# A hybrid attention, gMLP and mixture-of-experts step on one core: expert matrices laid row beside row on a partition

## What is computed

```python
def _hier_moe(h, router_group, router_expert, w_gate, w_up, w_down):
    t = h.reshape(B * L, D)                       # 640 tokens in all
    g_top, g_idx = lax.top_k(softmax(t @ router_group), 1)
    e_top, e_idx = lax.top_k(<expert logits of that group>, 2)
    weights = softmax(e_top) * g_top
    gates = <weights at the two chosen experts, 0 elsewhere>     # (640, 32)
    # w_gate, w_up: (32, 1024, 256)   w_down: (32, 256, 1024)
    hid = silu(einsum('td,edf->tef', t, w_gate)) * einsum('td,edf->tef', t, w_up)
    y = einsum('tef,efd->td', hid * gates[:, :, None], w_down)
```

## Time and profile before

| | |
|---|---|
| median of 3 runs | 660.07 us (659.71 to 664.84) |
| the profiled execution, its own time | 659.92 us |
| its span, first to last instruction | 658.1 us |
| TensorE matmul busy | 544.3 us (83%) |
| VectorE, ScalarE, POOL busy | 188.8, 151.6, 175.6 us |
| DMA | 173.15 MB in 53935 packets, mean 263 GB/s |
| mean granted TensorE clock | 0.957 of full speed |

### The profile page before, as it was taken

How to read it: one execution, slowest core, us unless ns; L and a number is a source line. 1 busy time by engine, 2 the same in 40 slices (tenths; PEclk the granted TensorE clock), 3 DMA queues, 4 the chain that set the end, 5 groups by cost and what they waited for, 6 DMA issues and landing times.

```text
span 658.1 us, 9133 instructions
## 1 busy us (share of the span) xinstructions
PE 544.3 (83%) x3051; PEld 297.7 (45%) x3051; DVE 188.8 (29%) x571; ACT 151.6 (23%) x374; POOL 175.6 (27%) x242
## 2 busy tenths in 40 slices
PE   0479999999988788999997889899998778897700
PEld 0235654444445455455553446465654334454400
DVE  1150222001176765144447411111111111111027
ACT  1630102001106655122223011111111111111133
POOL 1000000002422433033334533343343222221204
PEclk9999999999997999999999899999999898899965
DMA  7999207136099500442146799999999999999368
GB/s 238 405 403 397 107 1 271 49 122 262 1 264 410 223 2 1 168 165 82 65 169 246 262 346 394 409 407 412 403 397 404 389 393 397 400 413 411 142 276 218
DMA packets 53935, 173.15 MB, mean 263 GB/s; under 512 B 7740, under 2 KB 8420, under 8 KB 52976
## 3 DMA queue, kind: packets, MB, share of 16 engines
q1 hardware_dynamic: 45680, 153.88, 60.9%
q0 software_dynamic: 7184, 15.70, 7.3%
q10 hardware_dynamic: 1008, 2.75, 1.0%
HBM read 163.75 MB, written 16.68 MB: 274 GB/s over the span
## 4 chain that ended last, share of the span: by engine, by line
PE 46%; DMA 36%; DVE 7%; SPq 3%; ACT 3%; issue 3%; POOL 1%; POOLq 0%; DVEq 0%; ACTq 0%
DMA ring<-in_w_down_dram 17%; PE ps L714 11%; PE ps L611 10%; PE ps L592 5%; PE ps L513 5%; DMA w<-in_w_down_dram 5%; DMA w_6d<-in_w_down_dram 4%; PE ps L531 3%; PE ps L593 3%; DMA w_7d<-in_w_down_dram 2%; PE ps L861 2%; DMA ring<-in_w_mod_dram 2%; PE ps L691 2%; DMA ring<-in_w_up_dram 2%; SPq L424 2%
## 5 line engine op out<-in xcount | busy, mean ns | idle before, releaser
L861 PE MATMUL ps<-ring,xt 128*64 128x256 f32 x704 | 84.1, 393 | 14.6 <-DMA ring<-in_w_up_dram 9.5
L861 PEld LDWEIGHTS ps<-ring,xt 128*64 128x64 f32 x704 | 55.7, 141 | 49.2 <-DMA ring<-in_w_up_dram 15.7
L611 PE MATMUL ps<-ring,h_t 128*128 128x512 f32 x160 | 69.5, 593 | 0.0
L1354 DVE TENSOR_TENSOR hid<-act_g,ps 128x128 f32<-128x128 f32 x32 | 9.2, 288 | 196.6 <-ACT act_g L1572 196.6
L861 PE MATMUL ps<-w,xt 128*64 128x256 f32 x416 | 51.5, 401 | 10.5 <-DMA w<-in_w_up_dram 7.5
L714 PE MATMUL ps<-ring,mix_t 128*128 128x512 f32 x120 | 53.6, 596 | 0.0
L1698 POOL DMA_INDIRECT expert_results<-y_sb,idx_out x32 | 32.8, 1024 | 59.0 <-ACT y_sb L1586 49.8
L861 PEld LDWEIGHTS ps<-w,xt 128*64 128x64 f32 x416 | 33.6, 144 | 32.7 <-DMA w<-in_w_up_dram 12.2
L611 PEld LDWEIGHTS ps<-ring,h_t 128*128 128x128 f32 x160 | 30.1, 190 | 37.6 <-issue 37.6
L592 PE MATMUL ps<-ring,h_t 128*128 128x512 f32 x80 | 42.0, 607 | 2.7 <-DVE h_t L1013 2.7
L1629 POOL TENSOR_TENSOR gm_stats<-gm_stats,half_pow 128x8 f32<-128x8 f32 x5 | 9.7, 1941 | 129.4 <-DVE gm_stats L1079 129.4
(11 more groups left out here) (239 smaller groups left out, 723.9 us busy)
## 6 DMA issues: line engine op xcount, KB each, us to landing
ring<-in_w_mod_dram SPq DMA_DIRECT2D x8, 3072.0 KB, 19.6
ring<-in_w_gate_dram SPq DMA_DIRECT2D x20, 1024.0 KB
ring<-in_w_up_dram SPq DMA_DIRECT2D x20, 1024.0 KB
ring<-in_w_down_dram SPq DMA_DIRECT2D x20, 1024.0 KB
w<-in_w_gate_dram SPq DMA_DIRECT2D x12, 1024.0 KB
w<-in_w_up_dram SPq DMA_DIRECT2D x12, 1024.0 KB
y_back<-expert_results SPq DMA_DIRECT2D x5, 1024.0 KB, 8.7
ring<-in_w_in_dram SPq DMA_DIRECT2D x2, 2048.0 KB, 17.7
```

The costliest lines, as they stand in the source:

```text
L611: last = pe.matmul(ps[:, 4 + u % 4, :], h_t[:, k, i * P:(i + 1) * P], w[:, k, :], start=(k == 0), stop=(k == KC - 1))
L861: last = pe.matmul(bank[fh * SLOT:(fh + 1) * SLOT, 0:FE].rearrange("p (a f) -> p a f", a=2), x_t[:, k % 4, (k // 4) * SLOT:(k // 4 + 1) * ...
```

## The change

All three matrices of an expert are loaded as `(p k)`: partition p gets eight neighbouring rows of gate and of up (8p to 8p+7), and two neighbouring rows of down (2p and 2p+1), each in one run of 8 KB. Since partition p of chunk c of w_down is now row 2p+c, the hidden units are split into even and odd instead of first and second half: gate_up reads every second column. Chunk k of the model dimension is now every eighth, so `turn_x` takes every eighth column of a whole row. Tokens are gathered as whole rows: 64 indices, 4 KB each, on partitions 0 to 63 or 64 to 127 (four buffers in one tile of two rows; the fourth is that of the extra tiles). `turn_x` has eight transposes of 64 partitions x 128 columns. The buffers of the expert results change their places.

```diff
-        xg = sb("xg", [P, XS, 512], F32, a0)
-        xt = sb("xt", [P, 2, 4, P], F32, a0 + 6 * KB)
+        xg = sb("xg", [P, 2, D], F32, a0)
+        xt = sb("xt", [P, 2, KC, SLOT], F32, a0 + 8 * KB)
...
-        y_sb = sb("y_sb", [P, 2, 512], F32, a0 + 13 * KB)
+        y_sb = sb("y_sb", [P, 512], F32, a0 + 15 * KB)
...
-        xg_x = sb("xg_x", [P, 512], F32, b0 + 40 * KB)
-        y_sb2 = sb("y_sb2", [P, 512], F32, b0 + 42 * KB)
+        y_sb2 = sb("y_sb2", [P, 2, 512], F32, b0 + 40 * KB)
...
+        def x_rows(j):
+            return slice(SLOT * (j % 2), SLOT * (j % 2 + 1))
+        def x_buf(j):
+            return xg[x_rows(j), j // 2, :]
...
             def load_half(e, a):
-                sp.dma_start(weights(e)[0][:, a].rearrange("p (h k) f -> p h (k f)", h=2),
-                             (w_gate, w_up)[a][0, e].rearrange("(h p k) f -> p h (k f)", h=2, p=P)
+                sp.dma_start(weights(e)[0][:, a].rearrange("p k f -> p (k f)"),
+                             (w_gate, w_up)[a][0, e].rearrange("(p k) f -> p (k f)", p=P)
                              ).then_inc(wgu_in[e % LS], 16)
             def load_down(e):
-                sp.dma_start(weights(e)[1], w_down[0, e].rearrange("(k p) f -> p k f", p=P)).then_inc(wd_in[e % LS], 16)
+                sp.dma_start(weights(e)[1].rearrange("p k f -> p (k f)"), w_down[0, e].rearrange("(p k) f -> p (k f)", p=P)).then_inc(wd_in[e % LS], 16)
...
-            def turn_x(src, bank, done):
-                columns = src.rearrange("p (q k) -> p k q", k=4)
-                for cc in range(4):
-                    last = transpose(bank[:, cc * P:(cc + 1) * P], columns[:, cc])
+            def turn_x(j, bank, done):
+                columns = x_buf(j).rearrange("p (q k) -> p k q", k=KC)
+                for k in range(KC):
+                    last = pe.matmul(bank[:, k * SLOT:(k + 1) * SLOT], columns[:, k], ident[x_rows(j), x_rows(j)],
+                                     is_transpose=True, start=True, stop=True)
...
             def gate_up(x_t, w, bank, done):
                 for k in range(KC):
                     for fh in range(2):
                         last = pe.matmul(bank[fh * SLOT:(fh + 1) * SLOT, 0:FE].rearrange("p (a f) -> p a f", a=2),
-                                         x_t[:, k % 4, (k // 4) * SLOT:(k // 4 + 1) * SLOT],
-                                         w[:, :, k, fh * P:(fh + 1) * P], start=(k == 0), stop=(k == KC - 1))
+                                         x_t[:, k], w.rearrange("p a k (f c) -> p a k f c", c=2)[:, :, k, :, fh], start=(k == 0), stop=(k == KC - 1))
...
+            def token_index(dst, src):
+                return dve.tensor_scalar(dst, src, 1.0, float(NO_CODE), ALU.mult, ALU.add)
             dve.wait_ge(r_idx, 1)
-            row_index(idx_in[:, :, 0], ps[:, 6, 0:XS]).then_inc(rows_made, 1)
+            token_index(idx_in[:, :, 0], ps[:, 6, 0:XS]).then_inc(rows_made, 1)
...
             def gather(e):
                 j = e % XS
                 if e >= XS:
-                    pool.tensor_copy(idx_in[:, j, 0:1], src_row[:, e:e + 1]).then_inc(idx_cp, 1)
+                    pool.tensor_copy(idx_in[0:SLOT, j, 0:1], src_row[0:SLOT, e:e + 1]).then_inc(idx_cp, 1)
                     pool.wait_ge(idx_cp, e + 1 - XS)
-                pool.indirect_dma_start(xg[:, j, :], None, h2_halves,
-                                        bass.IndirectOffsetOnAxis(ap=idx_in[:, j, 0:1], axis=0),
-                                        bounds_check=2 * TILES * P - 1, oob_is_err=False).then_inc(xg_in[j], 16)
+                pool.indirect_dma_start(x_buf(j), None, h2_dram,
+                                        bass.IndirectOffsetOnAxis(ap=idx_in[0:SLOT, j, 0:1], axis=0),
+                                        bounds_check=TILES * P - 1, oob_is_err=False).then_inc(xg_in[j], 16)
...
-            pool.memset(xg_x[:], 0.0).then_inc(xg_zero, 1)
+            pool.memset(x_buf(XS), 0.0).then_inc(xg_zero, 1)
```

More of the change, by code:

```diff
@@ L169, in hybrid_dit_step @@
         mix_t = sb("mix_t", [P, KC, TILES * P], F32, a0)
-        xg = sb("xg", [P, XS, 512], F32, a0)
-        xt = sb("xt", [P, 2, 4, P], F32, a0 + 6 * KB)
-        act_g = sb("act_g", [P, 2, P], F32, a0 + 10 * KB)
-        hid = sb("hid", [P, 2, P], F32, a0 + 11 * KB)
-        hid_t = sb("hid_t", [P, 2, P], F32, a0 + 12 * KB)
-        y_sb = sb("y_sb", [P, 2, 512], F32, a0 + 13 * KB)
+        xg = sb("xg", [P, 2, D], F32, a0)
+        xt = sb("xt", [P, 2, KC, SLOT], F32, a0 + 8 * KB)
+        act_g = sb("act_g", [P, 2, P], F32, a0 + 12 * KB)
+        hid = sb("hid", [P, 2, P], F32, a0 + 13 * KB)
+        hid_t = sb("hid_t", [P, 2, P], F32, a0 + 14 * KB)
+        y_sb = sb("y_sb", [P, 512], F32, a0 + 15 * KB)
         act_x = sb("act_x", [P, P], F32, a0 + 17 * KB)
@@ L877, in next_x @@
                     pe.wait_ge(x_cp, e - 1)
-                turn_x(xg[:, e % XS], ps[:, e % 2, :], x_tr)
+                turn_x(e % XS, ps[:, e % 2, :], x_tr)
             def products(e):
@@ L907, in expert @@
                     pe.wait_ge(e_in, 16 * (x + 1))
-                    turn_x(xg_x[:, :], ps[:, xb, :], e_tr)
+                    pe.sem_inc(seen, 1)
+                    turn_x(XS, ps[:, xb, :], e_tr)
                     pe.wait_ge(e_cp, x + 1)
@@ L1331, in extra_rows @@
                 dve.wait_ge(r_idx, 3)
[L1332 removed]
+                token_index(src_row[:, EXPERTS:], ps[:, 6, 128:128 + N_X])
                 row_index(dst_row[:, EXPERTS:], ps[:, 6, 128 + N_X:128 + 2 * N_X]).then_inc(rows_made, 1)
```

18 lines of the change are left out of this document (8 added, 10 removed).

## The result

The changed kernel takes 677.39 us in the median (675.35 to 680.81) against 659.89 us (659.59 to 664.84) for the kernel before on the same chip: ratio 1.0252, interval 1.0188 to 1.0316. It is 2.5% slower. The forecast was 652.3 us, range 647 to 667. The span of the profiled execution is 675.4 us (before 658.1), its mean granted clock 0.959 (before 0.957).

What follows compares the result with a forecast made beforehand. DMA was taken as the bound, TensorE 22 us behind. Cheaper loads (-9.4), gathers (-1.0), start (+1.0) and longer turns put expert 30's product 8.6 us earlier; with +0.9 behind it, -7.7 gave 652.3 us, range 647 to 667.

Steps and rivals of the forecast that it cites:

- Gathers: Fetching an expert's 40 token rows whole instead of as halves: no change taken; bounds -1.0 us and +6 us.
- The -1.0 us for fewer runs: Gathers: one run of 4 KB a row instead of two of 2 KB, 0.04 us less an expert, over 25.
- Runs of 8 KB: Expert weight loads, half as many runs: 0.38 us less an expert, -9.4 us in all; bounds nothing and -9.4.
- Turn: Transposing tokens on TensorE, eight transposes instead of four: +0.4 us an expert; bounds +0.2 and +1.0.
- Products: Gate and up products reading every second column: taken as 0; bounds 0 and a doubling, +3.67 us each.
- Start: First turns and POOL's longer buffer clearing delay the first extra gather and the load of expert 5: +1.0 us.
- Tail: After the product of expert 30, turns of expert 31 and the last extra tile are uncovered: +0.9 us.
- The tie: At the product of expert 30, DMA arrives at 592.7 and TensorE at 593.1; 0.5 us more for taking turns.
- TensorE side: TensorE alone reaches the product of expert 30 at 593.1 us, from 580.0 plus the longer turns.
- Rivals: Other outcomes: no gain in loads (0.15), stepped reading slows products (0.18), turn costs more (0.10), a mixed case (0.15).
- between: Rival: both effects real, but TensorE and DMA hinder each other or gathers land unevenly: 653.5 to 660 us; chance 0.15.

Runs made afterwards that it cites:

- e1_rows_only: Kernel before with whole rows of 4 KB gathered by lists of 64 and eight transposes, matrices and products unchanged; 680.51 us, ratio 1.0256.
- e9_pairs2: Changed kernel gathering two experts' whole rows by one list of 128, token wait moved into the extra tile, ScalarE sharing the first eviction; 660.59 us, ratio 0.9967 to before.
- m1_gathers: Small kernel of only loads and gathers, each stage twelve 1 MB loads, most beside six 40-row gathers; 31.65 us without gathers, 40.04 with a list of 64.
- e4_down_only: Kernel before with only the new down matrix (8 KB runs) and products over every second column; 662.19 us, ratio 0.9982.
- e7_pairs: Changed kernel, but whole rows of two experts gathered by one list of 128 and eight full transposes for a pair; 669.74 us, ratio 1.0098 to before.
- e8_pairs_down_old: Changed kernel with two experts' whole rows gathered by one list of 128, plus the old down matrix and contiguous products; 664.35 us, ratio 1.0005 to before.
- e6_no_gather: Changed kernel whose gathers of the experts' tokens fetch only row 0 and skip all others, computing with wrong tokens; 651.42 us in one run.
- e11_list128: Changed kernel with two token buffers on partitions 0 to 63 and a list of 128 whose second half is out of bounds; 677.91 us, ratio 1.0225 to before.
- m4_map: Small kernel of transfers alone: two-row gathers and scatters at partitions 0 and x; with a list of 128, second row 159 ns or more behind for x = 1, 2, 3.
- e16_before_spread: Kernel before with one constant changed: the token of rank r takes slot 4 (r mod 16) + r / 16; 657.39 us, ratio 0.9917.

## Why the prediction was wrong, point by point

The forecast for the product of expert 30, gate_up(30), was 593.6 us; it came at 617.91. That is 24.3 of the 25 us by which the whole was off. Of these, 22 steps at 9.35 instead of 8.3 us are 23, and the start is 1.6.

- **Gathers: the step that failed.** "So I take no change", with a bound of +6 us. I knew that no view showed the dealing, and made up two maps, four and eight neighbouring partitions to an engine, that happened to give the same price. For before's half rows, 0.72 us, it was near the 0.64 measured, by luck. The list of 64, priced at 0.65, cost 1.40 us beside the loads where half rows cost 0.64: +0.76 us an expert, +19 us over 25. e1_rows_only shows it alone: +0.69 us a step. The bound was too small because it priced only the fullest engine, by a map that no row showed, and left out that the gather's rows could slow the weights' packets. The -1.0 us for fewer runs had nothing behind it either: two half rows on neighbouring partitions are already one packet of 4096 B (last section).
- **Runs of 8 KB: right mechanism, too large.** Packets halved, and one takes 309 to 312 ns as forecast. But 163.1 ns for 4 KB came from a busy share, which holds waiting as well; the median packet takes 159. By medians the gain is 7.63 - 7.42 = 0.21 us an expert, not 0.38, so -5 us instead of -9.4; 0.13 to 0.22 where it could be seen (e9_pairs2 against before, m1_gathers), and 0.01 where the down matrix alone was changed, a third of the weights (e4_down_only). The preference for packets of at most 4096 B in the Trainium skill ("DMA: Bandwidth & Descriptors", "SWDGE vs HWDGE vs iDMA"), which I weighed against the gain, did not bite: the weights went in packets of 8192 B, and 12 MB of them took 31.65 us against 32.55 in 4 KB runs.
- **Turn: right.** +0.45 us (1.10 against 0.65) for +0.4. Weight loads with a step of eight take 200 ns for 64 partitions and 193 for 128 (e9_pairs2), no more than with a step of four (207 for 128).
- **Products: taken as 0, measured +0.12 to +0.18 us.** A moving operand with a step of two is not free. It was hidden in the changed kernel, and decided in e7 against e8_pairs_down_old (5.4 us), where TensorE was the slower side.
- **Start: +1.0 forecast, +2.6 measured** (load of expert 5 at 380.83 against 378.27). First product +1.04 (367.04 against 366.00), POOL's clearing +0.42 (0.95 against 0.53), and the rest, 1.0, is the extra gather itself: from the end of its issue to the load are 3.48 us, before 2.49 (374.69 + 1.09 to 378.27).
- **Tail: +0.9 forecast, +1.6 measured.** From gate_up(30) to the end of the span 57.5 us; before 658.1 - 602.2 = 55.9.
- **The tie.** With free gathers (e6_no_gather, one run) there is no wait for loads at all between 400 and 600 us, gate_up(30) begins at 592.0 and the time is 651.4 us. So the forecast's TensorE side, 593.1, was about right, and 652 was about what the change gives when its gathers cost nothing, not its likeliest value.
- **Rivals.** None named the mechanism. "Gathers land unevenly" stood inside the case "between", at 653.5 to 660, with 0.15. Slower than 666.7 us had 0.25, but on TensorE's account, and the runs show DMA.

## What to carry to other kernels

A transfer by a list of 128 entries costs what its rows cost on the fullest DMA engine, not what its bytes cost on sixteen: with lists shorter than their slots, deal valid rows to different groups of four partitions, and check it by the step of the loads beside it. Keep such lists at 128 entries as well; a list of 64, 96 or 112 slows everything that moves beside it. The full length alone gives little (e11_list128): its rows have to lie on both halves of the partitions too (e7_pairs). When a change halves the number of packets of the large stream, price what it does to the small one with the same care: here 10% of the traffic took back more than the other 90% could gain.

## What the hardware did that I had not expected

- Six gathers of 40 neighbouring rows (list of 128) and six of 128 rows take the same time beside loads: 38.81 and 39.29 us a stage.
- Beside a list of 64 with 40 rows, 8 KB weight packets go from 316 to 350 ns in the mean, and the gather's own from 162 to 204.
- Two 2 KB rows of a list on neighbouring partitions are recorded as one packet of 4096 B (in m4_map rows at partitions 0 and 1 leave one record, at 0 and 2 two). From 405 to 597 us before's gathers and scatters are 1743 packets of 4 KB and 46 of 2 KB. So its half rows were already packets of 4 KB, and whole rows had nothing to gain.
- The DMA engines read as 101 to 102% busy in before and in e16_before_spread alike, 0.13 to 0.16 us a step apart: here a full share said nothing about how evenly they are loaded. That a packet's time includes waiting is my reading of it.
- A wait on TensorE ahead of a register load cost about 1 us behind it although the product that followed did not need it (e7_pairs, nine waits of 0.93 to 1.16 us; gone in e9_pairs2).
